# A hybrid decoder step on one core: norm statistics by token, another order of the first units, one more product pair, fewer passes for the sample tokens, and moved layer norm steps

## The chip, the core and the metric

The kernel runs on one core of one Trainium2 chip. The metric is the device time of one execution, in microseconds (us). In what follows PE is TensorE, DVE is VectorE, ACT is ScalarE, POOL is GpSimd and SP is SyncE, which here only issues loads and stores.

## What is computed

One layer of a decoder with four parallel branches, in fp32, over 1024 prompt tokens and 8 x 4 sample tokens (T = 1056 tokens, width 1024):

```python
h = rmsnorm(x, norm_g)
p = h @ w_in                                   # 1024 -> 16*512 + 8 + 4*1024 columns
# A: short gated convolution   B: retention, 4 heads, rotary q and k, head norm
# C: GLU, causal depthwise convolution of 31 taps, layer norm, swish
# D: mLSTM, 4 heads, exponential input gate, running-max stabiliser, head norm
y = x + (sum_n sigmoid(g_n(h)) * (o_n @ w_br[n])) @ w_out
out = rmsnorm(y, final_g)                      # and the new states of all branches
```

The samples carry their own states in, the prompt starts from zero, and all new states are outputs.

## The kernel before

**Numbers as two halves.** Every matmul operand is split into a high part (a copy rounded to fp32r, on ACT, line 1409 for weights) and a low part (the rest, by subtraction, on POOL, line 1739). A product is then three passes: high x high, high x low, low x high. The matrix of normalised tokens is `h_hi` and `h_lo`, 8 slices of channels by 1056 tokens.

**Start.** `x` comes in transposed, `xt`, in three blocks of 352 tokens. ACT squares it (line 1416), DVE (block 0, lines 1899 to 1903) or POOL (blocks 1 and 2, lines 1754 to 1758) adds up the 8 slices of channels, PE sums over partitions (`square_sums`, line 1045), ACT takes the root, DVE the reciprocal, and PE spreads that over all partitions (`spread_row`, line 1055). DVE multiplies (line 1911), ACT makes the high part (line 1427), DVE the low part (line 1884). `keep_busy` issues matmuls on constants between these steps.

**Units.** The input projection is done in units of 128 output channels. A unit is three blocks of 352 tokens, a block two halves of 12 matmuls (lines 1112 to 1114); the unit of the input and forget gates (`if`) has 16 small ones per block. A planner, `make_plan`, writes the order of everything: it counts half blocks, and a task stands at a number of half blocks within its phase. All engines walk the same list (`walk`), each in order and each doing only its own part, so that a task can make its engine wait while later work is queued behind it. The phases are: the gate unit and head 0 of the mLSTM (6 units, with the gate steps `m1` to `m7`, then the mask steps `mw` and `mws`), three more mLSTM heads, four retention heads, and a last one with the first GLU unit, a z unit and 4 plain gate units. During each phase the attention of the head before runs (`a`, `b`, `bs1`, `bs2`, `pn`, `pr`, `pt`): `a` transposes a chunk and makes scores, DVE masks them (line 2359), `b` (line 1282) multiplies them by the values, `pn` and `pr` normalise (line 2442), `pt` (line 1322) transposes back. `m1` is 9 transposes by matmul (line 1191), `m2` takes a logarithm on ACT, `m6` (lines 1218 to 1222) and a store and a broadcast load make the mask's row maxima, `mw` (line 2321) and `mws` (line 2329) the masks on DVE. The first `a` waits for all of them.

**Pairs.** The other input channels are done as 27 pairs of units: 7 products of half size (Winograd's form of Strassen's scheme) in place of 8, each in two parts, so 14 slots of 12 matmuls of 264 tokens (lines 1161 to 1163). Their sums are made on DVE, their sigmoids on ACT, and the weight sums on POOL. The operand sums of h (`comb`, `comb4`, lines 2161 to 2181) are made during the retention phases. Pair kinds are `cvcg` (GLU), `acau` and `abaz` (branch A), `cz` (branch C) and `g` (gates). In free slots DVE does the 120 steps of the 31-tap convolution (`tap`, line 2466), and from slot 263 of 378 on the layer norm (`ln0` to `ln3`, lines 2498 to 2534).

**End.** 32 branch units of 4 slices (`pblk`), summed into `acc`, then the final product by tiles of 128 tokens (lines 1367 to 1369): 8 prompt tiles and a ninth that covers the last 128 rows, of which only the 32 sample rows are stored. Each tile is added to x, normalised and stored.

Of the kernel before, what the change touches and what calls it, by code (L numbers as in the profile page):

```python
# [56 lines left out]
CK = BLK // 4  # L57
IFC, IFW = 8, 40
ORDER = (1, 3, 0, 2)
PLAIN_GATES = 4  # L60
# [12 lines left out]
def make_plan():  # L73
# [3 lines left out]
    def phase(group, tasks):  # L77
# [4 lines left out]
        if not first:  # L82

            blocks[:6] = [(u, b) for b in range(3) for u in range(2)]
# [66 lines left out]
    for x, step in zip((0, 1, 2, 4, 5, 6, 8, 9, 11, 13, 15, 17, 18, 20, 21), attention(7)):  # L151
# [5 lines left out]
    for k in range(4):  # L157
        tasks.setdefault(24 + 3 * k, []).append(("comb4", k))
# [30 lines left out]
    for what in (glu(1), None, conv_a(0), None, out_a(0), None, glu(2), None, conv_a(1), None, glu(3), None, out_a(1),  # L189
# [35 lines left out]
    for b in range(3):  # L225
        for late_by, step in ((0, "ln0"), (5, "lnm"), (6, "ln1"), (9, "ln1b"), (12, "lnv"), (13, "lns"), (15, "ln2")):
            tasks_at(at + 16 * b + late_by, (step, b))
    for g in range(4):
        tasks_at(at + 48 + 4 * g, ("ln3a", g))
        tasks_at(at + 50 + 4 * g, ("ln3", g))  # L230
    assert at + 50 + 12 <= 14 * 23 + 8, at
# [38 lines left out]
    emit_split(("plain", 1))  # L270
    emit_split(("plain", 0))
    start_steps = plan_out
    plan_out = []
    for s in first:
# [4 lines left out]
        if u + RING < n1:  # L279
            emit_split(("plain", u + RING))  # L280
        if u == n1 - 3:
            emit_split(("win", 0, 0))
        if u == n1 - 2:
            emit_split(("win", 0, 1))
            emit_split(("win", 0, 2))
        if u == n1 - 1:
            for i in range(3, 6):
# [4 lines left out]
    cycle = [4, 2 * r0, 2 * r0 + 1, 2 * r1, 2 * r1 + 1, 5]  # L292
# [92 lines left out]
def place(u, b):  # L385

    return 2 * b + u if u < 2 else 3 * u + b
# [151 lines left out]
def hybrid_step(nc, xT, xtok, ngain, wa, wg, wi, wb, wo, vec, fg, gbias, c1, c2, decay, rot, ah, chist, m0, st,  # L539
                y, sa_p, sa_s, sc_p, sc_s, o_p, o_s, om_p, om_s):  # L540
    ctx = ExitStack()
    with ctx:
# [51 lines left out]
        sq = [at(f"sq{i}", [P, KD, BLK], F32, acc_at + 4 * KD * BLK * i) for i in range(2)]  # L594
        rcol = at("rcol", [CK, 12], F32, acc_at + 8 * KD * BLK)
# [5 lines left out]
        buf_at = [x_at, x_at + 12 * T]  # L601
        zs_at = spot[0]
# [87 lines left out]
        lnsq = at("lnsq", [P, 4, BLK], F32, set_at)  # L690
# [29 lines left out]
        ident = cst[:, C_ID:C_ID + P]  # L720
        g_rows = nc.dram_tensor("g_rows", [4 * KD, P, T], F32, kind="Internal").ap()
# [3 lines left out]

        xt_in = [sem(f"xt_in{i}") for i in range(6)]
# [30 lines left out]
        ss_done = sem("ss_done")  # L757
        sqrt_done = sem("sqrt_done")
        pool_step = sem("pool_step")
        total = sem("total")  # L760
# [114 lines left out]

        def dst_of(item):
# [3 lines left out]
            if item[0] == "plain":  # L880
                return w_hi[item[1] % RING][:, :], w_lo[item[1] % RING][:, :]
# [68 lines left out]
        def _(sp):  # L950
# [8 lines left out]
            for i in range(6):  # L959
                b, k0 = i // 2, 4 * (i % 2)  # L960
                sp.dma_start(xt[:, b, k0:k0 + 4, :], xT[b, :, k0:k0 + 4, :]).then_inc(xt_in[i], 16)
                if i == 1:
                    sp.dma_start(ng[:, :], ngain).then_inc(ng_in, 16)
                    sp.dma_start(cst[:, :], c1).then_inc(ident_in, 16)
                    load(0, None)
                    load(1, None)
# [3 lines left out]
            load(2, 1)  # L970

            sp.wait_ge(row_ready, 3)
            sp.dma_start(cst2[:, :], c2).then_inc(late_in, 16)
            load(3, 0)
# [51 lines left out]
            for i in range(9):  # L1026
                r0 = i * P if i < 8 else T - P
# [1657 lines left out]
```

## Time and profile before

| | us |
|---|---|
| Median of 3 runs | 1505.76 (1505.31 to 1506.43) |
| The profiled execution | 1505.34, of which 1503.5 are the span of the profile |
| PE, DVE, ACT, POOL busy | 1475.7, 887.4, 498.6, 672.9 |

The share of the clock that PE was granted is 1 at 2.4 GHz and 0.5 at 1.2 GHz. A group of instructions has its own idle time and what ended it; the view of waits sums this by releaser. The chain of work is followed back from the last instruction to what released it at each step.

### The profile page before, as it was taken

To read this page: it belongs to the slowest core of one execution; us is meant where nothing else is said; L and a number is where in the kernel's file an instruction comes from. 1 tells how busy PE (TensorE), PEld (TensorE's weight loads), DVE (VectorE), ACT (ScalarE), POOL (GpSimd) and SP (SyncE) were. 2 spreads that over 40 slices of the span, in tenths; PEclk is the share of its full clock that TensorE was granted. 3 is DMA by queue.
4 is the path that set the end of the run, shared out by engine and by line. 5 is a ranking of instruction groups with operands and counts; after the bars stand their busy time and mean duration, and the time that the engine had idled before them with its cause. 6 is when DMAs were issued, how large, how long until landed. Compare 5 with 4: busy or idle time off the path is not lost.

```text
span 1503.5 us, 26633 instructions
## 1 busy us (share of the span) xinstructions
PE 1475.7 (98%) x10322; PEld 1436.6 (96%) x10322; DVE 887.4 (59%) x1770; ACT 498.6 (33%) x1010; POOL 672.9 (45%) x495
## 2 busy tenths in 40 slices
PE   7999999999999999999999999999999999999998
PEld 7999999999999999999999999999899999999786
DVE  5453342546766655448777877877666324785432
ACT  4432332323333334233333333333544422220321
POOL 5121212212131332387777776776667844662100
PEclk8999999999999999999999999999999999999999
DMA  4120212222121221322222221232222476755221
GB/s 163 61 99 29 87 35 81 75 70 67 52 89 45 72 77 50 114 65 90 72 102 89 89 89 68 62 99 86 87 87 100 144 235 202 232 159 158 100 86 72
DMA packets 64132, 144.41 MB, mean 96 GB/s; under 512 B 7800, under 2 KB 36488, under 8 KB 63880
## 3 DMA queue, kind: packets, MB, share of 16 engines
q1 hardware_dynamic: 56616, 116.12, 24.0%
q0 software_dynamic: 6192, 22.27, 4.1%
q10 hardware_dynamic: 1200, 4.33, 0.7%
q8 instruction: 82, 1.34, 0.4%
q14 instruction: 42, 0.34, 0.1%
HBM read 107.06 MB, written 35.64 MB: 95 GB/s over the span
## 4 chain that ended last, share of the span: by engine, by line
PE 92%; DVE 4%; POOL 1%; ACT 1%; issue 1%; DMA 0%; DVEq 0%; SPq 0%; ACTq 0%; POOLq 0%
PE bank L1161 11%; PE bank L1163 11%; PE bank L1162 11%; PE bank L1112 11%; PE bank L1114 10%; PE bank L1113 10%; PE bank L1179 4%; PE bank L1180 4%; PE bank L1181 4%; PE bank L1367 2%; PE bank L1368 2%; PE bank L1369 2%; PE sums_ps L1300 1%; PE sums_ps L1267 1%; PE sums_ps L1282 1%; PE sums_ps L1286 1%
## 5 line engine op out<-in xcount | busy, mean ns | idle before, releaser
L1112 PE MATMUL bank<-h_hi,w_hi 128*128 128x352 f32 x1008 | 335.2, 333 | 0.0
L1114 PE MATMUL bank<-h_hi,w_lo 128*128 128x352 f32 x1008 | 325.0, 322 | 0.0
L1113 PE MATMUL bank<-h_lo,w_hi 128*128 128x352 f32 x1008 | 324.4, 322 | 0.0
L1739 POOL TENSOR_TENSOR w_lo<-stage,w_hi 128x1024 fp32r<-128x1024 f32 x44 | 105.9, 2406 | 371.3 <-ACT w_hi L1409 371.2
L1739 POOL TENSOR_TENSOR t_lo<-stage,t_hi 128x512 fp32r<-128x512 f32 x140 | 185.9, 1332 | 135.5 <-ACT t_hi L1409 135.4
L1161 PE MATMUL bank<-h_hi,t_hi 128*128 128x264 f32 x864 | 246.4, 285 | 0.0
L1162 PE MATMUL bank<-h_lo,t_hi 128*128 128x264 f32 x864 | 245.5, 284 | 0.0
L1163 PE MATMUL bank<-h_hi,t_lo 128*128 128x264 f32 x864 | 245.0, 284 | 0.0
L1112 PEld LDWEIGHTS bank<-h_hi,w_hi 128*128 128x128 f32 x1008 | 190.1, 189 | 1.0
L1113 PEld LDWEIGHTS bank<-h_lo,w_hi 128*128 128x128 f32 x1008 | 190.6, 189 | 0.0
L1161 PE MATMUL bank<-c_hi,t_hi 128*128 128x264 f32 x648 | 185.7, 287 | 4.8 <-DVEq L2153 3.1
L1114 PEld LDWEIGHTS bank<-h_hi,w_lo 128*128 128x128 f32 x1008 | 189.9, 188 | 0.0
L1163 PE MATMUL bank<-c_hi,t_lo 128*128 128x264 f32 x648 | 184.7, 285 | 0.0
L1162 PE MATMUL bank<-c_lo,t_hi 128*128 128x264 f32 x648 | 184.0, 284 | 0.0
L2466 DVE SCALAR_TENSOR_TENSOR sums_ps<-ext,vc,sums_ps 128x1024 f32<-128x1024 f32 x116 | 149.0, 1284 | 44.5 <-ACT sums_ps L1654 40.9
L1409 ACT ACTIVATE t_hi<-stage 128x512 fp32r<-128x512 f32 x140 | 87.8, 630 | 226.3 <-PE bank L1181 100.2
L1162 PEld LDWEIGHTS bank<-h_lo,t_hi 128*128 128x128 f32 x864 | 162.5, 188 | 0.3
L1161 PEld LDWEIGHTS bank<-h_hi,t_hi 128*128 128x128 f32 x864 | 162.4, 188 | 0.3
L1163 PEld LDWEIGHTS bank<-h_hi,t_lo 128*128 128x128 f32 x864 | 162.4, 188 | 0.0
L1739 POOL TENSOR_TENSOR t_lo<-wsum,t_hi 128x512 fp32r<-128x512 f32 x81 | 109.2, 1350 | 83.1 <-ACT t_hi L1409 83.0
L1161 PEld LDWEIGHTS bank<-c_hi,t_hi 128*128 128x128 f32 x648 | 122.3, 189 | 6.1 <-DVEq L2153 3.4
L1179 PE MATMUL bank<-o_hi,t_hi 128*128 128x352 f32 x384 | 124.1, 323 | 0.0
(360 smaller groups left out, 2853.1 us busy)
## 6 DMA issues: line engine op xcount, KB each, us to landing
stage<-in_wa SPq DMA_DIRECT2D x64, 512.0 KB, 3.3
piece<-g_rows SPq DMA_DIRECT2D x96, 176.0 KB, 2.9
stage<-in_wg SPq DMA_DIRECT2D x32, 512.0 KB, 3.8
g_rows<-sgt SPq DMA_DIRECT2D x112, 132.0 KB, 1.8
o_raw<-o_rows SPq DMA_DIRECT2D x16, 528.0 KB, 6.5
stage<-in_wb SPq DMA_DIRECT2D x32, 256.0 KB, 2.8
xr<-in_xtok SPq DMA_DIRECT2D x9, 512.0 KB, 3.5
xt<-in_xT SPq DMA_DIRECT2D x6, 704.0 KB, 6.7
```

The source lines that it names most:

```text
L1112: pe.matmul(out, hi, h_hi[:, k, tok(b)], start=(k == 0), stop=False)
L1113: pe.matmul(out, hi, h_lo[:, k, tok(b)], start=False, stop=False)
L1114: mm = pe.matmul(out, lo, h_hi[:, k, tok(b)], start=False, stop=(k == KD - 1))
L1161: pe.matmul(out, hi, a_hi(k), start=(first and k == 0), stop=False, skip_group_check=True)
L1162: pe.matmul(out, hi, a_lo(k), start=False, stop=False, skip_group_check=True)
L1163: mm = pe.matmul(out, lo, a_hi(k), start=False, stop=(k == 3), skip_group_check=True)
L1179: pe.matmul(out, hi, o_hi[n][:, k, tok(b)], start=(k == 0), stop=False)
L1180: pe.matmul(out, hi, o_lo[n][:, k, tok(b)], start=False, stop=False)
L1181: mm = pe.matmul(out, lo, o_hi[n][:, k, tok(b)], start=False, stop=(k == 3))
L1409: act.activation(dst_of(item)[0], split_src(item), ACT.Copy).then_inc(hi_done, 1)
L1739: pool.tensor_tensor(lo, split_src(item), hi.bitcast(F32), ALU.subtract).then_inc(lo_done, 1)
L2466: own(dve.scalar_tensor_tensor(cc[g][:, 0:TP] if k == CW - 1 else conv_ps, ext[g % 2][:, k:k + TP], vc[:, g, V_CW + k:V_CW + k + 1], conv_ ...
```

## The change

- **Norm of x.** x is loaded a second time, by token (`xk`, chunks of 128, 128 and 96 tokens), ahead of `xt`. ACT squares and sums each chunk in one instruction; the sums on DVE and POOL and `square_sums` are gone. `spread_row` has 3 pieces instead of 4, for block 1 after the first `if` block and for block 2 after block 0 of unit 2.
- **First units.** Units 0, 1 and 2 are interleaved by block (before: 0 and 1); unit 2 gets a third weight buffer, in the still empty `qkv`.
- **Gate steps.** `m1`'s transposes are split into three of 3 chunks. The steps stand at half blocks 14 to 29 (before 10 to 24), the masks at 32 to 35 (before 28 to 32). The attention of head 0 starts at half block 2 with a stride of 1.5 (before 1 and 1.55).
- **Moved sums.** `comb` in the retention phases at half blocks 16 to 21 (before 3 to 19). In the last phase head 7's last steps, and `comb4`, come sooner.
- **Gates.** 2 plain gate units instead of 4; the other two are one more pair, the first of now 28.
- **Layer norm.** It starts at slot 252 of 392, with 20 slots per block of tokens (before 16), and one square buffer is split in two places. The convolution's steps are spread over the slots again.
- **Normalisation of heads.** Line 2442 becomes a `scalar_tensor_tensor` with a broadcast column.
- **Final product.** The sample tile is third, its high and low parts stand side by side as 64 columns of weights, and it has two passes instead of three.

```diff
-PLAIN_GATES = 4
+PLAIN_GATES = 2
-            blocks[:6] = [(u, b) for b in range(3) for u in range(2)]
+            blocks[:9] = [(u, b) for b in range(3) for u in range(3)]
-    gates = {10: [("m1",)], 11: [("m2",)], 14: [("m3",)], 15: [("m4",)], 19: [("m5",)], 22: [("m6",)], 24: [("m7",)]}
+    gates = {14: [("m0", 0)], 15: [("m0", 3)], 16: [("m0", 6), ("m1",)], 17: [("m2",)], 19: [("m3",)], 20: [("m4",)], 24: [("m5",)],
+             27: [("m6",)], 29: [("m7",)]}
     for c in range(0, CH, 2):
-        gates[28 + c // 2] = [("mw", c), ("mw", c + 1)]
-    gates[32] = [("mws",)]
+        gates[32 + c // 2] = [("mw", c), ("mw", c + 1)]
+    gates[35].append(("mws",))
...
-            phase(mlstm(1), spread(attention(0), 1, 1.55))
+            phase(mlstm(1), spread(attention(0), 2, 1.5))
...
-            for i, x in enumerate((3, 7, 11, 13, 16, 19)):
+            for i, x in enumerate((16, 18, 19, 20, 20, 21)):
                 tasks.setdefault(x, []).append(("comb", h - 1, i))
             for c in range(3):
-                tasks.setdefault((20, 22, 23)[c], []).append(("comb_split", h - 1, c))
+                tasks.setdefault((22, 23, 23)[c], []).append(("comb_split", h - 1, c))
...
-    for x, step in zip((0, 1, 2, 4, 5, 6, 8, 9, 11, 13, 15, 17, 18, 20, 21), attention(7)):
+    for x, step in zip((0, 1, 2, 4, 5, 6, 8, 9, 11, 13, 15, 16, 17, 18, 19), attention(7)):
...
-        tasks.setdefault(24 + 3 * k, []).append(("comb4", k))
+        tasks.setdefault((20, 22, 24, 26)[k], []).append(("comb4", k))
...
-    for what in (glu(1), None, conv_a(0), None, out_a(0), None, glu(2), None, conv_a(1), None, glu(3), None, out_a(1),
+    for what in (None, glu(1), None, conv_a(0), None, out_a(0), None, glu(2), None, conv_a(1), None, glu(3), None, out_a(1),
...
-        for late_by, step in ((0, "ln0"), (5, "lnm"), (6, "ln1"), (9, "ln1b"), (12, "lnv"), (13, "lns"), (15, "ln2")):
-            tasks_at(at + 16 * b + late_by, (step, b))
+        for late_by, step in ((0, "ln0"), (6, "lnm"), (7, "ln1"), (10, "ln1b"), (14, "lnv"), (15, "lns"), (17, "ln2")):
+            tasks_at(at + 20 * b + late_by, (step, b))
...
+            by_token(0)
+            by_channel(0)
+            sp.dma_start(cst[:, :], c1).then_inc(ident_in, 16)
+            sp.dma_start(ng[:, :], ngain).then_inc(ng_in, 16)
+            load(0, None)
+            by_channel(1)
+            load(1, None)
+            by_token(1)
+            by_channel(2)
+            load(2, 0)
+            by_channel(3)
+            by_token(2)
...
             pe.wait_ge(ones_set, 1)
-            keep_busy(20)
-            square_sums(0)
-            keep_busy(3)
+            keep_busy(24)
             spread_row(0)
-            keep_busy(14)
-            square_sums(1)
+            keep_busy(22)
...
+            def square(b, j):
+                act.wait_ge(xk_in[3 * b + j], 16)
+                n, c = XCH[j], 3 * b + j
+                act.activation(xk[b % 2][0:n, j, :], xk[b % 2][0:n, j, :], ACT.Square,
+                               accum_out=rcol[0:n, c:c + 1]).then_inc(sq_done, 1)
...
-                    own(dve.tensor_scalar(rt[0:r, c, 0:P], rt[0:r, c, 0:P], mv[0:r, c, 0:1], rstd[0:r, c:c + 1],
-                                          ALU.subtract, ALU.mult))
+                    own(dve.scalar_tensor_tensor(rt[0:r, c, 0:P], rt[0:r, c, 0:P], mv[0:r, c, 0:1],
+                                                 rstd[0:r, c:c + 1].to_broadcast([r, P]), ALU.subtract, ALU.mult))
...
+        by_turn = (0, 1, CH) + tuple(range(2, CH))
...
+                        if by_turn[i] == CH:
+                            pe.matmul(out[0:2 * NS, :], f_two[:, k, :], hi, start=(k == 0), stop=False)
+                            mm = pe.matmul(out[0:2 * NS, :], f_two[:, k, :], lo, start=False, stop=(k == KD - 1))
+                            continue
```

## Rows read from the trace of the kernel before

**Rows 1.** The page, part 1: busy time, share of the span, instructions.

```profile
PE 1475.7 (98%) x10322; PEld 1436.6 (96%) x10322; DVE 887.4 (59%) x1770; ACT 498.6 (33%) x1010; POOL 672.9 (45%) x495
```

**Rows 2.** Waits of PE: line, releaser, us in total, times, longest.

```profile
PE sums_ps L1045 <- DVE sq L1903: 4.3, 1, 4.3
PE sums_ps L1045 <- POOL sq L1758: 3.6, 1, 3.6
PE bank L1161 <- DVEq L2153: 3.1, 1, 3.1
PE sums_ps L1282 <- DVE sw L2359: 3.1, 4, 1.0
PE sums_ps L1322 <- DVEq L2445: 1.9, 1, 1.9
PE bank L1161 <- DVE part L2026: 1.7, 2, 1.1
```

**Rows 3.** Stretches: length, busy time (instructions) by engine, granted clock, DMA share, GB/s.

```profile
25.00:30.00 5.00, 5.00 (x28) 4.03 (x27) 1.45 (x4) 1.52 (x2) 4.84 (x4) 0.66 0.30 105
50.00:55.00 5.00, 5.00 (x23) 5.00 (x23) 0.20 (x1) 2.67 (x3) 1.21 (x1) 0.68 0.33 107
1060.00:1070.00 10.00, 6.86 (x43) 6.31 (x42) 8.67 (x16) 2.11 (x5) 3.87 (x4) 0.85 0.35 107
```

**Rows 4.** Stretches of one plain unit, one pair, one final tile, columns as above.

```profile
625.70:637.10 11.40, 11.40 (x73) 11.40 (x73) 0.00 (x0) 2.86 (x5) 5.87 (x4) 1.00 0.42 141
955.60:976.00 20.40, 20.40 (x171) 20.40 (x170) 16.44 (x27) 6.67 (x14) 14.61 (x12) 1.00 0.23 66
1452.60:1463.80 11.20, 11.20 (x50) 9.05 (x49) 3.97 (x5) 2.51 (x4) 0.00 (x0) 1.00 0.27 94
```

**Rows 5.** The chain at the start: start us, us, what.

```profile
1.20 5.30 DMA xt<-in_xT
...
8.93 0.53 DVE sq L1901
9.49 2.56 DVE sq L1903
...
25.26 0.20 PE bank L1098
```

**Rows 6.** Instructions at the start in order of time: start us, us, instruction.

```profile
4.77 1.38 ACT L1416 ACTIVATE sq<-xt 128x1408 f32<-128x1408 f32 x1 [2.34 <-DMA xt<-in_xT]
...
9.32 2.34 POOL L1739 TENSOR_TENSOR w_lo<-stage,w_hi 128x1024 fp32r<-128x1024 f32 x1 [7.12 <-ACT w_hi L1409]
...
16.48 4.02 DVE L1911 SCALAR_TENSOR_TENSOR xt<-xt,ng,sums_ps 128x352 f32<-128x352 f32 x8 [2.60 <-PE sums_ps L1055]
```

**Rows 7.** Instructions of the gate and mask steps, in order of time.

```profile
46.98 2.10 PE L1191 MATMUL sums_ps<-sel,gif 40*128 40x8 f32 x18
...
53.73 1.28 ACT L1502 ACT_TABLE_LOAD   x1
...
75.82 1.03 PE L1222 MATMUL sums_ps<-dms,cst 4*128 4x8 f32 x8
...
88.77 2.43 DVE L2321 SCALAR_TENSOR_TENSOR wt<-wt,aa,cst 128x128 f32<-128x128 f32 x8
...
102.00 0.71 DVE L2329 SCALAR_TENSOR_TENSOR wts<-sums_ps,aa,cst 32x32 f32<-32x32 f32 x4 [0.51 <-DVE wt L2321]
...
106.50 0.27 PE L1263 MATMUL sums_ps<-cst,qkv 128*128 128x128 f32 x1
```

**Rows 8.** The chain in a retention phase.

```profile
402.81 0.71 DVE c_raw L2161
```

**Rows 9.** The chain in the abaz pair.

```profile
1059.95 2.38 DVE sums_ps L2522
```

**Rows 10.** Stores of y, two stretches: KB each, median us from issue to landing.

```profile
out_y<-yo ACTq DMA_DIRECT2D x1, 512.0 KB, 2.6
...
out_y<-yo ACTq DMA_DIRECT2D x1, 128.0 KB, 1.9
```

More of the change, by code:

```diff
@@ L269, in make_plan @@
     push_loads()
-    emit_split(("plain", 1))
-    emit_split(("plain", 0))
+    for n in range(3):
+        emit_split(("plain", n))
     start_steps = plan_out
@@ L385, in place @@
 def place(u, b):
[L387 removed]
+    return 3 * b + u if u < 3 else 3 * u + b
 def done_counts():
@@ L723, in hybrid_step @@
         nm_row = nc.dram_tensor("nm_row", [CH * HEADS, P], F32, kind="Internal").ap()
+        xk_in = [sem(f"xk_in{i}") for i in range(9)]
         xt_in = [sem(f"xt_in{i}") for i in range(6)]
@@ L1039, in keep_busy @@
                     pe.matmul(bank[4][:, 0:P], ones[:, :], ones[:, :], start=True, stop=True)
-            def square_sums(b):
-                pe.wait_ge(total, b + 1)
-                for j in range(4):
-                    mm = pe.matmul(tb[0:CK, 4 * b + j:4 * b + j + 1], sq[b % 2][:, 0, CK * j:CK * j + CK], ones[:, 0:1],
-                                   start=True, stop=True)
-                mm.then_inc(ss_done, 1)
             def spread_row(b):
@@ L1053, in spread_row @@
                 pe.wait_ge(recip_done, b + 1)
-                for j in range(4):
-                    mm = pe.matmul(rows[b][:, CK * j:CK * j + CK], rcol[:, 4 * b + j:4 * b + j + 1].to_broadcast([CK, P]),
-                                   ident[0:CK, 0:CK], start=True, stop=True)
+                for j in range(3):
+                    n = XCH[j]
+                    mm = pe.matmul(rows[b][:, P * j:P * j + n], rcol[0:n, 3 * b + j:3 * b + j + 1].to_broadcast([n, P]),
+                                   ident[0:n, 0:n], start=True, stop=True)
                 mm.then_inc(row_ready, 1)
             pe.wait_ge(ones_set, 1)
-            keep_busy(20)
-            square_sums(0)
-            keep_busy(3)
+            keep_busy(24)
             spread_row(0)
-            keep_busy(14)
-            square_sums(1)
+            keep_busy(22)
             last = {}
@@ L1427, in upper @@
                 act.activation(h_hi[:, ks, tok(b)], xt[:, b, ks, :], ACT.Copy).then_inc(hh_done, 1)
-            act.wait_ge(ones_set, 4)
+            act.wait_ge(ones_set, 5)
             own(act.activation(ss[:, 0, 1:2], eps[:, :], ACT.Sqrt))
-            square(0)
-            square(1)
+            for j in range(3):
+                square(0, j)
+            root(0)
             split(0)
-            root(0)
-            square(2)
-            square(3)
+            upper(0, 0)
             split(1)
-            upper(0, 0)
             upper(0, 1)
+            square(1, 0)
             upper(0, 2)
-            square(4)
+            square(1, 1)
+            square(1, 2)
             root(1)
-            square(5)
+            split(2)
+            square(2, 0)
             upper(1, 0)
+            square(2, 1)
             upper(1, 1)
+            square(2, 2)
+            upper(1, 2)
             root(2)
-            upper(1, 2)
             for i in range(3):
@@ L1914, in _ @@
                         mul.then_inc(hn_dve, 1)
-                lower(b, 0)
-                lower(b, 1)
-                if b == 1:
-                    reciprocal(2)
-                lower(b, 2)
-                if b == 0:
-                    reciprocal(1)
+                for i in range(3):
+                    lower(b, i)
+                if b < 2:
+                    reciprocal(b + 1)
             dve.wait_ge(const_in, 48)
```

198 lines of the change are left out of this document (96 added, 102 removed).

## The prediction

> **What bounds the kernel now.** Read part 1 of the page first: TensorE is busy for 1475.7 of 1503.5 us, and no other engine for more than 59% of it [rows 1]. So time is won in two ways only: fewer TensorE columns, or shorter TensorE waits. The waits by releaser come next: two waits on the norm at the start of 4.3 and 3.6 us, 3.1 on VectorE's scores in four places, 3.1 in one piece and 1.7 in two (the longer 1.1) at products of pairs, and 1.9 at an attention head's transpose [rows 2]. The third view is the stretches with the granted clock: at 25 to 30 us, 50 to 55 us and 1060 to 1070 us it is 0.66, 0.68 and 0.85, that is 2.4 GHz falls to 1.2 GHz for part of them [rows 3]. Each follows idleness or tiny matmuls: the first the wait for the norm of block 1, the second the 18 matmuls of 8 columns of the gate step [rows 7], the third the 3.1 us wait. The loss is (1 - clock) x length: 1.7, 1.6 and 1.5 us. Last, what a unit costs: a plain unit takes 11.4 us, a pair 20.4 us, a tile of the final product 11.2 us, all at full clock [rows 4].
>
> **1. Start: 12.5 us less.** Before, the first product starts at 25.26 us [rows 5]. After, the order of loads decides. Two loads of 704 KB land 1.74 us apart, with the first there at 4.77 and the second at 6.50 [rows 5, 6], so the flow begins near 3.0 and takes 2.5 us per 1000 KB. Token chunks of 512, 512 and 384 KB land at 4.3, 5.6, 6.5; x by channel at 8.2 and 10.2; the first ring weight at 11.5; block 1 by token at 12.8 to 15.0, by channel at 16.7 and 19.7. A square of 1408 columns takes 1.38 us [rows 6], one of 1024 by its length 1.0, with its sum about 1.1, so the third ends at 7.8, the root at 8.0. The 48 warm-up matmuls end near 8.7, the row is spread by 9.5. VectorE's eight multiplies take 4.02 us [rows 6]: 13.5. ScalarE splits unit 1's weight at 12.2 to 13.2, and GpSimd's half of it runs 13.3 to 15.7. Here I chose. VectorE's first lower half wants to start at 13.5, while GpSimd is subtracting. In the trace such an add of 352 columns took 2.56 us from 9.49 on, beside a GpSimd subtraction of 9.32 to 11.66, where the one before it took 0.53 [rows 5, 6]. I take the blocked value: the lower half ends at 16.6, the first product starts at 16.7, 8.6 us sooner; free, 14.7. The Trainium skill (SBUF — State Buffer, Who interferes with whom) says that a VectorE instruction with two SBUF inputs and a GpSimd one that reads SBUF exclude each other, the first to issue going first; the 2.56 us agrees. By that rule the 0.2 us between 13.3 and 13.5 decides 2 us.
> Nothing after it should stop TensorE: with three units per block there are 2.6 + 3.9 + 3.9 us of products to hide the 8 us of the next block's norm, and blocks 1 and 2 come at 28.6 and 38.9, h_lo ready at 27.7 and 36.0. So the clock loss of 1.7 us at 25 to 30 goes. The gate transposes in three parts of 6 tiny matmuls (2.1 us in all, as before) between full products: the 1.6 us at 50 to 55 go as well. The matmuls for square sums go, and the spread has 9 pieces for 12: 0.6 us. Together 8.6 + 1.7 + 1.6 + 0.6 = 12.5. Bounds 9 (the wait of 14.3 to 16.7 halves the clock, and a late load) to 14.5.
>
> **2. The gate steps come closer together: 2.8 us more.** A half block is 1.93 us. Between the second and third gate step there were three halves, now two; ScalarE there does a split and two table loads of 1.28 us [rows 7], about 4.5 us in all against 3.9: 0.7 us of waiting, and 0.3 at the next, where VectorE now has the sigmoid of the z unit ahead of it. Then the mask: the sixth step's matmuls end at 76.85, the broadcast of the row maxima is in for VectorE at 88.77, the sample mask is done at 102.7, and the first attention tile starts at 106.50 [rows 7]. That is 25.9 us of chain in 29.7 us of products: 3.8 spare. After, the sixth step moves from half 22 to 27 and the tile from 37 to 38: 11 halves instead of 15, about 22.2 us. The chain loses a copy (0.65) and perhaps the blocked instruction in it (about 1.9): 23.4 to 25.3. TensorE waits 1.2 to 3.1 us there; I take 1.8, since GpSimd's next subtraction starts only near the chain's end. Behind this wait stand all of TensorE's units, so it is paid in full. Sum 0.7 + 0.3 + 1.8 = 2.8; bounds 1 to 6 (with a clock fall). Start and gates: 9.7 us won.
>
> **3. Sums of h moved in the retention phases: 2.1 us.** In three phases VectorE does a sum of 0.71 us [rows 8] between rotation and the scores for which TensorE waits [rows 2]. At halves 16 to 21 it lies in VectorE's idle time before the transposes. 3 x 0.71 = 2.1; bounds 1 to 2.2, since the rotation's own blocked add stays.
>
> **4. Last attention head: 2.0 us.** The transpose waited 1.9 us for VectorE's normalisation [rows 2], which had begun late because ScalarE did a split and a table load ahead of its root, and whose first instruction GpSimd blocked. Now the root is at half 16, ahead of the split, one half sooner; the transpose comes two halves sooner. From 1.9 us of wait about zero stays: ready at 601, wanted at 601.3. Bounds 0 to 2.2. The other form of that instruction (scalar_tensor_tensor) I count as nothing: 9 per head behind other work.
>
> **5. Two gate units become a pair: 2.5 us.** 2 x 11.4 - 20.4 = 2.4 to 2.5 [rows 4]. Its sums and sigmoids lie beside other work: VectorE was busy 16.44 of 20.4 us in a full pair [rows 4].
>
> **6. Layer norm: 6.0 us.** At 1059.95 VectorE's reciprocal of 2.38 us [rows 9] and four multiplies sit in the abaz pair before the parts that free TensorE's banks: 3.1 us waited [rows 2] and 1.5 us of clock [rows 3], about 5.0 with the restart of the queue. Later the mean of the third block costs 0.6, since VectorE's sum for it stands right behind a reciprocal, and in the cz pair the last step of the layer norm stands ahead of a product's sum, 1.1 waited [rows 2] and 0.3 of restart. Together about 7. After, by the slots, block 0 lies in the acau and the gate pair, block 1's reciprocal at slot 9 of abaz, three slots sooner. Adding up VectorE's queue there (4.2 us of reciprocal and multiplies, 0.43 each for some ten operations, 1.6 for the next sum) the last bank is freed 26.0 us after the pair's start, and wanted at 25.7: 0.3 us. In the gate pair VectorE has 20.5 us of work in 20.4: another 0.3 to 0.8. I leave 1.0 of 7.0. Bounds 2 (b below) to 7.
>
> **7. Final product: 3.0 us.** The sample tile has 32 matmuls instead of 48; a matmul takes 11.2 / 48 = 0.233 us [rows 4]: 3.7 us. It also goes third, so the last store is 512 KB and not 128: 2.6 against 1.9 us to landing [rows 10], 0.7 back. VectorE's four more instructions (0.7 each) hide under 7.4 us of products.
>
> **Sum:** 9.7 + 2.1 + 2.0 + 2.5 + 6.0 + 3.0 = 25.3 us. The profiled execution took 1505.34 us (1503.5 span and 1.8 around it), so 1480.0 by it; the median shown is 0.4 above: 1480.4.
>
> **Rivals.**
> (a) The attention tile's wait decides. The chain of step 2 is blocked (25.3 us), the idleness of 3 us brings the clock down as the 3.1 us wait did [rows 2, 3], and the wait at 14.3 us does so too: 1.3 + 1.6 + 1.7 more, and about 1485. Against it: the 1.9 us wait at the last head left the clock alone.
> (b) VectorE is still too full around abaz: the layer norm moves its wait from one pair to the next and keeps 4 to 5 of the 7 us, 1484. For it: 79 to 80% busy in full pairs before a layer norm step is added.
> (c) VectorE goes first in the collision at 13.5 and the mask chain is not blocked: 2 + 1 less, 1477.
> (d) On the other side: VectorE becomes the bound of the pairs. From 20.4 us of its work per pair each further us is paid once in each of 28 pairs; the fullest had 16.44 [rows 4]. Taps now sit closer from the first pair on and keep a pair from recovering; 21.4 us in every pair would cost 28 us and give about 1508. The same taps in more slots speak against it.
> (e) The norm by token brings nothing: x is read twice, and if the 1408 KB ahead of x by channel cost what the squares' sums did, the first product stays at 25: about 1489. Against it: before, two thirds of the 25 us went to squares' sums on three engines, after both first loads were in at 6.5 [rows 5].
>
> **Chances.** Forecast (1478 to 1482.5) 0.45; (a) 0.17; (b) 0.14; (c) 0.13; (e) 0.06; (d) 0.02; several small ones at once, 1486 to 1492, 0.03. The range 1475.5 to 1487.5 takes in all but some 0.12 of it. Faster by over 0.2% (what a measurement of this kernel can tell from none, 3 us) 0.97, within 0.01, slower 0.02.
>
> **What would show it.** First product near 16.7 us and no clock below 1 before 60 us. A wait at the first attention tile, with VectorE's sample mask as releaser. No wait of scores over 0.6 us in the three phases; none at the last head's transpose. In the abaz pair under 1 us. 28 pairs of 20.4 us and 41 units ahead of them. The last store issued 2.6 us before the end. Wrong would be the whole if VectorE or a split became a releaser of many small TensorE waits in the pairs.

## The result and the profile after

The changed kernel takes 1498.43 us (median of 4 runs, 1498.03 to 1499.24), the kernel before 1506.1 beside it (median of 4): a ratio of 0.9949, interval 0.9936 to 0.9961. It is faster by 7.7 us, where 25.3 were forecast. The profiled execution took 1499.24 us with a span of 1497.5, 6.0 less than the profiled one before; the table below takes these 6.0 us apart.

Where the 25.3 us went is read from the starts of TensorE's stages in the two traces. A minus sign means that the stretch became longer.

| stretch | forecast, us won | measured |
|---|---|---|
| start and gate steps (to the tenth plain unit, 164.4 before, 158.7 after) | 9.7 | 5.7 |
| retention phases (the next units to 599.4 before, 592.2 after) | 2.1 | 1.5 |
| last attention head (to the end of the unit after z, 614.2 and 611.4) | 2.0 | -4.4 |
| two gate units as a pair (22.9 us against 20.4) | 2.5 | 2.5 |
| pairs beyond 20.4 us each (27 pairs before, 28 after) | 6.0 | -2.1 |
| final product | 3.0 | 2.8 |

Three of the six lines came out within 0.6 us, the first fell 4.0 short, and the last head and the pairs ended on the other side of zero. The pairs' line is the time from the first product of pairs to the last (562.4 and 584.9 us) less 20.4 for each pair. The page, part 1, of after, which answers to [rows 1]:

```profile
PE 1468.2 (98%) x10318; PEld 1427.2 (95%) x10318; DVE 901.7 (60%) x1779; ACT 504.3 (34%) x1031; POOL 669.9 (45%) x495
```

TensorE has 7.5 us less of busy time, and is still busy for 98% of the span. Its waits by releaser (line, releaser, us in total, times, longest), which answer to [rows 2]:

```profile
PE bank L1182 <- DVEq L2160: 5.1, 1, 5.1
PE sums_ps L1345 <- DVEq L2452: 4.6, 2, 3.7
PE bank L1119 <- DVE h_lo L1902: 2.5, 1, 2.5
PE sums_ps L1079 <- DVE rcol L1907: 2.4, 1, 2.4
PE bank L1182 <- DVE part L2033: 1.3, 2, 0.7
PE sums_ps L1305 <- DVE sw L2366: 1.2, 4, 0.3
PE sums_ps L1305 <- ACTq L1576: 1.2, 1, 1.2
...
PE sums_ps L1220 <- DVEq L2234: 0.8, 1, 0.8
```

The wait at the abaz pair, 3.1 us before, is 5.1 (first line), and the one at the last head's transpose, 1.9 before, is 3.7 in one piece (second line; the other 1.0 of it is the first head's). The scores' waits fell from 3.1 to 1.2, as forecast. The granted clock (columns as in [rows 3]) is whole in the two stretches at the start where it fell before the change, and falls behind the two long waits:

```profile
10.00:30.00 20.00, 16.70 (x119) 15.35 (x118) 15.71 (x22) 13.72 (x22) 5.72 (x4) 1.00 1.02 375
50.00:60.00 10.00, 9.66 (x61) 9.01 (x60) 0.91 (x4) 5.41 (x7) 4.76 (x2) 1.00 0.17 55
...
595.00:605.00 10.00, 7.05 (x29) 6.60 (x30) 5.12 (x10) 1.52 (x3) 6.08 (x5) 0.66 0.30 105
...
1060.00:1072.00 12.00, 6.86 (x33) 6.14 (x32) 8.47 (x15) 0.97 (x3) 7.63 (x8) 0.72 0.44 136
```

That is 3.4 us lost to 1.2 GHz at either place. Two stretches of after in order of time show what VectorE did there. c_lo is the lower half of a sum of h, w_lo that of a unit's weight, t_lo that of a pair's. The last head:

```profile
591.60 6.24 DVE L2449 SCALAR_TENSOR_TENSOR rt<-rt,mv,rstd 128x128 f32<-128x128 f32 x9
592.12 0.54 POOL L1789 DMA_DIRECT2D out_o_p<-cn  x1
592.68 1.35 POOL L1809 TENSOR_TENSOR c_lo<-c_raw,c_hi 128x528 fp32r<-128x528 f32 x1
...
593.98 2.40 POOL L1770 TENSOR_TENSOR w_lo<-stage,w_hi 128x1024 fp32r<-128x1024 f32 x1
...
597.95 1.97 PE L1345 MATMUL sums_ps<-cst,rt 128*128 128x128 f32 x8 [3.66 <-DVEq L2452]
```

The nine normalising instructions take 6.24 us; in the first seven heads the same nine take 2.44. One by one they are 0.35, 0.35, 2.06, 2.43, and five of 0.34. Two are stretched: the third ends 0.16 us after c_lo, the fourth 0.16 us after w_lo. By the profile the third begins at 592.13, 0.55 us ahead of c_lo; starts on GpSimd are rough, so that c_lo is what held it is inferred from where it ends. The abaz pair:

```profile
1055.30 0.42 DVE L2052 TENSOR_TENSOR ta<-bank,ta 128x264 f32<-128x264 f32 x1
1055.64 1.17 DVE L2054 TENSOR_TENSOR ta<-part,ta 128x264 f32<-128x264 f32 x1
...
1058.68 1.52 DVE L2505 TENSOR_TENSOR lnsq<-cc,cc 128x352 f32<-128x352 f32 x1
1060.12 1.58 DVE L2506 TENSOR_TENSOR lnsq<-cc,cc 128x352 f32<-128x352 f32 x1
1061.74 1.47 DVE L2508 TENSOR_TENSOR lnsq<-lnsq 128x352 f32<-128x352 f32 x1
```

```profile
1055.04 1.48 POOL L1770 TENSOR_TENSOR t_lo<-stage,t_hi 128x512 fp32r<-128x512 f32 x1
1058.52 2.80 POOL L1770 TENSOR_TENSOR t_lo<-stage,t_hi 128x512 fp32r<-128x512 f32 x2 [2.00 <-ACT t_hi L1436]
1061.29 1.54 POOL L1770 TENSOR_TENSOR t_lo<-wsum,t_hi 128x512 fp32r<-128x512 f32 x1
```

The three adds of the layer norm's block 2 take 1.5 us each; the adds of blocks 0 and 1 take 0.52. Beside them GpSimd makes three lower halves. In the first two rows a multiply with one operand in PSUM (bank) runs its 0.42 us in the middle of a lower half, and the next, of the same size with both in SBUF, takes 1.17.

The whole trace of after says the same. Of VectorE's tensor_tensor instructions with both operands in SBUF, 93 ran beside an elementwise instruction of GpSimd and 65 of these were stretched by over 0.15 us; of 134 that ran clear of it, none was. With an operand in PSUM 364 ran beside it, and none was stretched by more than 0.02 us (counted over instructions that occur at least three times, against their usual time).

### The profile page after: what moved, and what is told of

It is laid out like the page before. It is cut to its first block, busy times and chain, and to the rows that moved or that the text cites. A ratio compares the mean times of both kernels' runs of the same rounds, so it can differ in the third digit from the quotient of the medians.

```text
span 1497.5 us, 26690 instructions
## 1 busy us (share of the span) xinstructions
PE 1468.2 (98%) x10318; PEld 1427.2 (95%) x10318; DVE 901.7 (60%) x1779; ACT 504.3 (34%) x1031; POOL 669.9 (45%) x495
## 4 chain that ended last, share of the span: by engine, by line
PE 88%; DVE 6%; DMA 2%; ACT 2%; issue 1%; POOL 1%; SPq 0%; DVEq 0%; ACTq 0%; POOLq 0%
PE bank L1182 12%; PE bank L1184 11%; PE bank L1183 11%; PE bank L1133 10%; PE bank L1135 9%; PE bank L1134 9%; PE bank L1200 4%; PE bank L1201 4%; PE bank L1202 4%; PE bank L1394 1%; PE bank L1396 1%; PE bank L1395 1%; PE sums_ps L1290 1%; PE sums_ps L1305 1%; PE sums_ps L1309 1%
## 5 line engine op out<-in xcount | busy, mean ns | idle before, releaser
L1133 PE MATMUL bank<-h_hi,w_hi 128*128 128x352 f32 x960 | 320.1, 333 | 0.0
L1135 PE MATMUL bank<-h_hi,w_lo 128*128 128x352 f32 x960 | 309.8, 323 | 0.0
L1134 PE MATMUL bank<-h_lo,w_hi 128*128 128x352 f32 x960 | 309.1, 322 | 0.0
L1182 PE MATMUL bank<-h_hi,t_hi 128*128 128x264 f32 x896 | 255.5, 285 | 0.0
L1183 PE MATMUL bank<-h_lo,t_hi 128*128 128x264 f32 x896 | 254.6, 284 | 0.0
L1184 PE MATMUL bank<-h_hi,t_lo 128*128 128x264 f32 x896 | 254.1, 284 | 0.0
L1133 PEld LDWEIGHTS bank<-h_hi,w_hi 128*128 128x128 f32 x960 | 181.1, 189 | 1.1
L1134 PEld LDWEIGHTS bank<-h_lo,w_hi 128*128 128x128 f32 x960 | 181.6, 189 | 0.0
L1135 PEld LDWEIGHTS bank<-h_hi,w_lo 128*128 128x128 f32 x960 | 180.9, 188 | 0.0
L1183 PEld LDWEIGHTS bank<-c_lo,t_hi 128*128 128x128 f32 x672 | 127.3, 189 | 0.5 <-issue 0.2
```

The lines of the kernel that those rows point to most:

```text
L1133: pe.matmul(out, hi, h_hi[:, k, tok(b)], start=(k == 0), stop=False)
L1134: pe.matmul(out, hi, h_lo[:, k, tok(b)], start=False, stop=False)
L1135: mm = pe.matmul(out, lo, h_hi[:, k, tok(b)], start=False, stop=(k == KD - 1))
L1182: pe.matmul(out, hi, a_hi(k), start=(first and k == 0), stop=False, skip_group_check=True)
L1183: pe.matmul(out, hi, a_lo(k), start=False, stop=False, skip_group_check=True)
L1184: mm = pe.matmul(out, lo, a_hi(k), start=False, stop=(k == 3), skip_group_check=True)
```

## The experiments

The theory after the result: GpSimd's subtractions hold VectorE's instructions that have both operands in SBUF, and the changed kernel puts two groups of them at places where GpSimd works and TensorE waits. All edits are to the changed kernel. Gains are counted from its median of 1498.43 us unless another is named; times of the executions of one kernel spread by 1 to 5 us. Readings of single rows are from the profiled execution of each run.

**e1: the last head's transposes later.**

```
-    ... 13, 15, 16, 17, 18, 19), attention(7)):
+    ... 13, 15, 16, 17, 20, 21), attention(7)):
-    tasks.setdefault((20, 22, 24, 26)[k], []).append(("comb4", k))
+    tasks.setdefault((22, 23, 25, 27)[k], []).append(("comb4", k))
```

> The changed kernel with one edit: the two transpose steps of the last attention head lie at half blocks 20 and 21 of their phase, as before, instead of 18 and 19 (the sums of its four tiles follow at 22, 23, 25, 27, since their buffers overlap). Its normalisation stays at half 16. Theory (the steps came sooner than VectorE can normalise there, since GpSimd's c_lo and w_lo hold it): TensorE arrives at 597.8, VectorE is done at 597.84, so the wait of 3.7 us falls under 0.3 and the 6.8 us at 1.2 GHz behind it go too (3.0 us): 1498.4 - 6.5 = 1491.9. Rival 1 (the clock fall does not come from this wait): 3.7 less, 1494.7. Rival 2 (the later sums of tiles hold the first pair): the same gain less 1 to 3 us of a new wait at 622, 1493 to 1495.

Measured: 1493.93 us (1493.22 to 1497.77), 4.5 less where the theory said 6.5; this is in the range of rival 2. In the trace the nine instructions still took 6.30 us, nobody waited for them, and the pairs begin at 616.9 instead of 622.9: 6.0 us, wait and clock fall. Behind that rival 2 came too, but smaller than its 1 to 3 us: the first pair's wait for L2033 grew from 0.6 to 1.3 us. That the median gained less than the trace may come from executions of the changed kernel in which the clock did not fall there (e9); it is not shown.

**e2: the form of the instruction.**

```
-    own(dve.scalar_tensor_tensor(rt..., rt..., mv[0:r, c, 0:1], rstd[0:r, c:c + 1].to_broadcast([r, P]), ...))
+    own(dve.tensor_scalar(rt..., rt..., mv[0:r, c, 0:1], rstd[0:r, c:c + 1], ALU.subtract, ALU.mult))
```

> The changed kernel with one edit: the nine normalising instructions per head in their form of before (tensor_scalar with two scalars per partition, instead of scalar_tensor_tensor with a broadcast SBUF operand). Theory (the place beside GpSimd's c_lo and w_lo decides, not the form; in the kernel before one tensor_scalar of this group took 2.07 us there): nine pieces of the last head still take 4 to 6.3 us, wait 3.7 and clock fall stay, 1498.4 within 1 us. Rival (the second SBUF operand is what gets blocked): the nine take 2.4 to 3 us, end at 594.5, wait about 0.5, no clock fall: 1498.4 - 6.2 = 1492.

Measured: 1497.74 us. The row of the nine in its trace:

```profile
591.43 6.10 DVE L2449 TENSOR_SCALAR rt<-rt,mv,rstd 128x128 f32<-128x128 f32 x9
```

6.10 against 6.24, two of them 2.01 and 2.38, where 2.06 and 2.43 stood. The form of the instruction makes no difference here, as the prediction had counted it.

**e3: the layer norm off the abaz pair.**

```
+    late_by += (0, 5 if step == "ln2" else 0, 3)[b]
```

and the closing steps three slots later.

> The changed kernel with the layer norm moved off the abaz pair: the last step of block 1 (reciprocal and four products) five slots later, in the gate pair behind, and all steps of block 2 and the closing steps three slots later. Theory (VectorE's work of the layer norm in the abaz pair makes the wait of 5.1 us at 1060 and the 6.8 us at 1.2 GHz): both go, 8.5 us, and up to 1 us comes back in the gate pair: 1490 to 1491. Rival (VectorE is too full in any pair there): a wait of 2 to 4 us stands in the gate pair instead, with its clock fall: 1494 to 1497.

Measured: 1497.22 us, 0.2 above the rival's range, and by its mechanism: the wait for the abaz pair's bank (L2160) is gone, and 4.1 us are waited for a product's sum in the gate pair behind, with a clock fall. The reciprocal and the adds of block 2 now stand next to each other there, and the adds again run beside GpSimd (columns: start, us, instruction):

```profile
1063.19 1.10 DVE L2506 TENSOR_TENSOR lnsq<-cc,cc 128x352 f32<-128x352 f32 x1
1064.04 1.37 POOL L1758 TENSOR_TENSOR wsum<-wsum,stage 128x512 f32<-128x512 f32 x1
1064.22 1.58 DVE L2507 TENSOR_TENSOR lnsq<-cc,cc 128x352 f32<-128x352 f32 x1
...
1065.83 1.47 DVE L2509 TENSOR_TENSOR lnsq<-lnsq 128x352 f32<-128x352 f32 x1
```

So it was not the abaz pair as such. The first of the three (1.10 for 0.52) ran beside GpSimd's instruction of 1062.38 to 1063.90, which is an add of two half weights, so not only subtractions hold VectorE.

**e4: the three adds alone.**

```
+    late_by += 3 if (step, b) == ("ln0", 2) else 0
```

> The changed kernel with a single step moved: the channel sums of block 2 (three VectorE adds) three slots later, out of the abaz pair; the reciprocal and the products of block 1 stay at its slot 9. Theory (the collision decides: three adds of 1.5 us beside GpSimd's lower halves, 0.52 elsewhere): the queue is 4.6 us shorter, the wait of 5.1 falls to 0.5 to 1.0, no clock fall, 1490.5 to 1491.5, and the three adds take 0.52 each or are blocked where nobody waits. Rival (the reciprocal and products of 4.2 us fill the queue and the adds count only with their own 1.6): a wait of about 3.5 us and the clock fall stay, 1496.8.

Measured: 1493.78 us (1492.93 to 1496.6), 4.6 less where 7 to 8 were forecast; in the trace the 28 pairs take 5.7 us less, with the clock whole. At their new place the adds ran 0.55, 0.51 and 0.52 us, and the reciprocal with its products, unmoved, leaves a wait of 0.4. The matmul that needs the adds now waits 1.3 us, which accounts for the gap between the trace and the forecast, not for that between the median and the trace.

**e13: GpSimd's work cut, nothing moved.**

```
+    n = 16 if item in (("plain", NU - 1), ("win", 21, 4), ("win", 21, 5), ("win", 21, 6)) else hi.shape[-1]
-    pool.tensor_tensor(lo, split_src(item), hi.bitcast(F32), ALU.subtract)
+    pool.tensor_tensor(lo[..., 0:n], split_src(item)[..., 0:n], hi[..., 0:n].bitcast(F32), ALU.subtract)
```

> The changed kernel with four of GpSimd's subtractions cut to 16 columns: w_lo of the last plain unit (2.40 us, 593.98 in the trace of after) and the three t_lo of 1058.5 to 1062.8 (1.3 to 1.5 us each). Nothing of VectorE's or TensorE's work and no place of a step is changed; the lower halves of those weights are left out but for 16 columns. c_lo (1.35 us, ahead of w_lo) stays. Theory (GpSimd's subtractions hold VectorE's instructions): at the last head the third of the nine pieces is still held by c_lo (2.0 us), the fourth falls from 2.43 to 0.35, the wait from 3.7 to 1.8 us; the three adds of block 2 fall from 1.5 to 0.52 each, the wait from 5.1 to about 2.2; with the clock falls of 6.8 us gone or halved 1498.5 - 4.9 - 3 to 6 = 1488 to 1491. Rival (VectorE is slow there for itself, or beside ScalarE): pieces and adds keep their length, 1498.5.

Measured: 1490.46 us (the kernel before 1505.82 beside it), 8 less. The rows:

```profile
592.16 4.17 DVE L2450 SCALAR_TENSOR_TENSOR rt<-rt,mv,rstd 128x128 f32<-128x128 f32 x9
...
593.24 1.36 POOL L1810 TENSOR_TENSOR c_lo<-c_raw,c_hi 128x528 fp32r<-128x528 f32 x1
594.54 0.29 POOL L1771 TENSOR_TENSOR w_lo<-stage,w_hi 128x16 fp32r<-128x16 f32 x1
```

```profile
1054.62 0.53 DVE L2506 TENSOR_TENSOR lnsq<-cc,cc 128x352 f32<-128x352 f32 x1
1055.06 0.54 DVE L2507 TENSOR_TENSOR lnsq<-cc,cc 128x352 f32<-128x352 f32 x1
1055.64 0.53 DVE L2509 TENSOR_TENSOR lnsq<-lnsq 128x352 f32<-128x352 f32 x1
```

One of the nine is still held (2.07), beside the c_lo that was left; the one held by w_lo is free (0.34). The adds are 0.53. The waits are 1.6 and 2.2 us where 1.8 and 2.2 were expected; behind the second the clock still fell, and 1.7 us were lost. This shows the cause: the same VectorE work stood in the same places, and only GpSimd's was taken away. It agrees with the Trainium skill (SBUF — State Buffer, Who interferes with whom), by which a VectorE instruction with two SBUF inputs contends with a GpSimd one that reads SBUF, and the one that issues second is fully blocked; the page names tensor_scalar among those that can contend, and in e2 it was held.

**e7: the layer norm's spacing undone.** Stride 16 for 20, offsets (0, 5, 6, 9, 12, 13, 15).

> The changed kernel with the layer norm spaced as before (16 steps from block to block, offsets 0, 5, 6, 9, 12, 13, 15), in the new order of pairs. The reciprocal of block 1 then lies at slot 3 and the adds of block 2 at slot 4 of the abaz pair. What the prediction said (the wider spacing brings 6 us): 1504. Theory (what counts is whether a step lies ahead of a bank's release beside GpSimd's subtractions, not the spacing): waits of 2 to 4 us in that pair instead of 5.1 and less of a clock fall, 1495 to 1499.

Measured: 1501.85 us (11 executions, 1499.72 to 1504.89; the profiled one took 1503.2), between the two expectations and above the theory's. There are two waits in gate pairs, both with a clock fall: 3.5 us at a product (1022), behind a reciprocal and adds held for 1.12, 1.59 and 1.47 us, and 3.1 at a matmul of the variance (1065), whose sums VectorE brings late; no run takes the second apart further. So the new spacing did win 3.4 us in the new order of pairs, and the order itself had lost more: beyond 20.4 us each, the pairs take 11.6 us before, 17.5 with the old spacing in the new order, 13.7 in the changed kernel.

**e11: the place of the added pair.**

```
-    for what in (None, glu(1), None, ... out_a(3), None, None, None, out_c(0), ...
+    for what in (glu(1), None, ... out_a(3), None, None, None, None, out_c(0), ...
```

> The changed kernel with a single edit: the added pair of gate units stands before the two cz pairs, not at the head of the pairs. Taps and layer norm then fall on the pairs as before the change: of the layer norm the abaz pair holds the mean, squares and variance of block 0, and both the reciprocal and the adds of the next block come in the gate pair behind it. Theory (where the steps meet the abaz pair's releases decides; the place of the added pair put them there): 28 pairs take 571.2 plus 5 to 9 us instead of plus 13.7: 1490 to 1494. Rival (in any pair the reciprocal with the adds behind it makes a wait of 3 to 5 us and a clock fall): 1497 to 1500.

Measured: 1494.87 us, 3.6 less and 0.9 above the theory's range. The 28 pairs take 571.2 plus 10.0 us: 3.7 less than in the changed kernel, by one line in a list, but 1 us more than expected. A wait of 2.6 us stays in the gate pair behind the abaz pair.

**e12 and e14: what that wait is.** e12 is e11 with the three edits of e5, e6 and e1 (sums of tiles at 22, 23, 24, 26); e14 is e12 with the adds of blocks 1 and 2 two slots later.

> The first three edits of the combination (start, gates, last head) with the added pair before the cz pairs in place of the layer norm's moved steps. Theory: 1498.4 - 11.2 and the gain of the pair's place as the run with that edit alone shows it, 4 to 8 us: 1479 to 1483. Rival (the collision comes back in the gate pair): 1486.

> The combination with the added pair ahead of the cz pairs, and the channel sums of the layer norm's blocks 1 and 2 two slots later. In the combination without it the three adds of block 1 take 1.4 to 1.6 us each behind the reciprocal, beside GpSimd, and make a wait of 2.9 us at 1031 with 3.4 us at 1.2 GHz behind it. Theory: two slots later the adds stand behind the products' sums, so the wait falls under 0.5 and the clock stays: 1484.2 - 4.3 = 1479.9. Rival (GpSimd works there as well, and the adds are held two slots later at the next bank): 1483 to 1484.

Measured: 1484.17 and 1480.34 us. e12 lies 1.2 us above the theory's range: the place of the pair brought 3.7 us and not 4 to 8, since the wait of 2.6 us and its clock fall stay. There the adds stand ahead of the sum that TensorE waits for:

```profile
1028.92 1.41 DVE L2508 TENSOR_TENSOR lnsq<-cc,cc 128x352 f32<-128x352 f32 x1
...
1030.26 1.60 DVE L2509 TENSOR_TENSOR lnsq<-cc,cc 128x352 f32<-128x352 f32 x1
...
1031.89 1.47 DVE L2511 TENSOR_TENSOR lnsq<-lnsq 128x352 f32<-128x352 f32 x1
...
1033.62 0.43 DVE L2036 TENSOR_TENSOR part<-bank,part 128x264 f32<-128x264 f32 x1 [0.25 <-DVE lnsq L2511]
```

In e14 both sums of that step are done at 1031.1, the adds behind them are still held (1.06, 1.61 and 1.50 us), and there is no wait: a held instruction costs only what stands behind it.

**e5: the norm of block 2 later.** `spread_row(2)` after (0, 1) for (2, 0); ScalarE's `upper(1, i)` ahead of `square(2, i)`.

> The changed kernel with two edits in the start: TensorE spreads the norm of block 2 after the gate unit's product of block 1 instead of before it, and ScalarE copies the three parts of block 1's h ahead of the squares of block 2 instead of between them. Theory (the wait of 2.7 us at 28.9 is the norm of block 2, asked for 2.6 us before it can be there, since its token rows land at 24.6 to 28 us): the wait goes, at most 0.3 us stands at the new place: 1498.4 - 2.4 = 1496.0. Rival (the loads of x, now taken twice, bound the start: the products of block 2 find their h_lo late instead): the wait reappears there, 1498 to 1498.4.

Measured: 1498.5 us, by the time alone no gain, and the number is the rival's. By the trace the theory holds: the wait is gone and none stands in its place, every later stage begins 2.4 us sooner (the pairs at 620.5 for 622.9), and the profiled span is 1495.1 for 1497.5. Two things in e9 can hide this in the median, and no run separates them: the clock at the last head, and that the wait itself is 0.9 us and not 2.4 in some executions.

**e9: the changed kernel again.**

> The changed kernel unedited, as a base on the same chip for the three runs beside it: 1498.4 within 1.5 us, with the waits of 2.7 us at 28.9, 4.0 at 594 and 5.4 at 1060 in their places.

Measured: 1499.09 us, but 1495.85 to 1499.82. The 1495.85 is the profiled run, and in it the wait at the last head is there (3.6 us) without the fall of the clock. The wait for the norm of block 2 is 0.9 us there and not the 2.7 that was expected: behind the wait of 2.5 us for the first product, which both traces have, the clock fell in this one, which lost 1.7 us, and TensorE came to the norm that much later (columns as in [rows 3]):

```profile
18.00:24.00 6.00, 6.00 (x31) 4.63 (x30) 2.88 (x6) 2.51 (x4) 1.72 (x1) 0.72 1.04 403
```

The tenth plain unit begins at 158.6 us in it and at 158.7 in after, so this fall cost nothing as long as the norm was late anyway. The stretch 590 to 605 us in after, in e6 and in e9:

```profile
590.00:605.00 15.00, 11.34 (x56) 10.61 (x55) 9.86 (x18) 5.58 (x10) 9.51 (x8) 0.77 0.30 110
```

```profile
590.00:605.00 15.00, 11.06 (x63) 10.51 (x62) 8.62 (x14) 2.75 (x6) 9.64 (x8) 0.89 0.32 124
```

```profile
590.00:605.00 15.00, 11.36 (x72) 10.82 (x72) 9.79 (x18) 5.46 (x9) 9.61 (x8) 1.00 0.29 111
```

Clock 0.77, 0.89 and 1.00 of full behind waits of 3.7, 3.9 and 3.6 us: 3.4, 1.7 or 0 us lost. A single edit of 2 us can be lost in that unless the trace is read.

**e6: gate steps.** m3, m4 at 20, 21 for 19, 20; the first head's steps at 2, 4, 5, 7, ... for 2, 3, 5, 6, ..., its transposes at 22 and 23.

> The changed kernel with the third and fourth gate step one half block later (20, 21), the scores' step of the first attention tile one half later behind its first step (4 for 3), and the transposes of that head one half later (22 for 21, 23 stays). Theory (three small waits of the closer gate phase: 0.8 us at 59.3 for two activation tables in a row, 1.2 at 103.6 for ScalarE's table between the mask's exponential and the tile's sigmoid, 1.0 at 152.4 for the normalisation): all three go with their restarts, 1498.4 - 3.3 = 1495.1. Rival (the chain of the masks is the bound, and the later third step pushes it): 0.8 and 1.0 go, but 1 to 2 us appear at the first tile: 1497.

Measured: 1494.57 us, 3.9 less (3.3 were forecast). All three waits are gone and none came; the tenth plain unit begins 3.5 us sooner. The pairs begin 4.6 us sooner, in which the shorter clock fall of its profiled run has a part (1.7 us less, the rows under e9).

**e8: the sums of h at their old halves.**

> The changed kernel with the combinations of h in the three retention phases at their halves of before. Prediction's term and theory agree: a sum of 0.70 us lies between the rotation and the scores again, three times: +1.9 to 2.1, 1500.4, with the waits for scores at about 1.3 instead of 0.66 us. Rival (the moved sums were hidden anyway, and the shorter wait has another cause): 1498.4.

Measured: 1500.80 us. The scores' waits are 3.1 us again, three of them 0.96 for 0.34 us, and the pairs begin 2.0 us later: the term is right.

**e10: the four together.** e5, e6, e1's transposes (sums of tiles at 22, 23, 24, 26), the adds of block 2 three slots later and its other steps one.

> Four edits of the changed kernel together: the norm of block 2 spread one product later with ScalarE's copies ahead of its squares; gate steps 3 and 4, the first tile's scores and that head's transposes one half block later; the last head's transposes at 20 and 21 with its sums of tiles at 22, 23, 24, 26; the layer norm's channel sums of block 2 three slots later and its other steps one later. Theory (four separate waits, each by work of VectorE or ScalarE asked for too soon; the gains add): by the starts of the pairs 2.4 + 3.6 + 5.2, and 6.5 in the layer norm: 1498.4 - 17.7 = 1480.7, clock at 1.2 GHz nowhere between 20 us and the end. Rival (a gain in one place moves GpSimd's subtractions in the next into a new collision): one of the four comes back, 1484 to 1487.

Measured: 1481.24 us (1480.93 to 1481.77), ratio to the kernel before 0.9837, interval 0.9823 to 0.985. Its clock and busy time from 20 us to the end of the last product, and its waits:

```profile
20.00:1475.00 1455.00, 1447.08 (x10212) 1408.61 (x10210) 887.52 (x1756) 490.72 (x1010) 664.83 (x484) 1.00 0.30 97
```

```profile
PE bank L1123 <- DVE h_lo L1906: 2.5, 1, 2.5
PE bank L1186 <- DVE part L2037: 2.1, 2, 1.4
PE sums_ps L1309 <- DVE sw L2370: 1.2, 4, 0.3
...
PE bank L1186 <- DVEq L2164: 0.4, 1, 0.4
```

The clock is whole in this stretch but for its first 2 us, the end of a fall behind the first product's wait that the mean hides. The gains add as the traces had them: 17.9 us less than the changed kernel beside it, 17.7 expected, while the medians of e1, e4, e5 and e6 alone add up to 12.9. e14 is as fast or a little faster, 1480.34 us, 0.983 (0.9816 to 0.9843): a version 18 us below the changed kernel and 25.5 below the one before. That this is the 1480.4 that was forecast is chance: it took further edits that the prediction did not have.

## Why the prediction was wrong

1. **Start: mechanism right, about 4 us too much.** The clock falls at 25 and 50 us went, as forecast. The first product came at 17.9 us, not 16.7: the collision with w_lo came as priced (the first lower half took 3.24 us for 3.1), but the third chunk of rows had landed at 7.7 us for 6.5. The step that failed is "nothing after it should stop TensorE". The spread of block 2's norm stands behind the third unit's product of block 0, and TensorE reaches it at 29.2, while the prediction timed only the products' need of h_lo. The rows of after:

```profile
24.64 1.06 ACT L1442 ACTIVATE xk<-xk 128x1024 f32<-128x1024 f32 x1 [2.29 <-DMA xk<-in_xtok]
...
31.57 0.91 PE L1079 MATMUL sums_ps<-cst,rcol 128*128 128x128 f32 x6 [2.38 <-DVE rcol L1907]
```

The three chunks of block 2 land at 24.6, 26.3 and 28.1 us. The prediction's 2.5 us per 1000 KB from 3.0 us on would give 23.7 for the third (8260 KB with those ahead of it), so the rate was too fast as well: measured, it is 3.0. ScalarE's copies of block 1's h stand between the squares and add to it. e5 takes 2.4 us of it back. About 1 us of the 4 is not traced.
2. **Gate steps: size nearly right, places partly wrong.** 0.7, 0.3 and 1.8 us were forecast. The third step waited 0.8. At the first tile's first step nothing was waited, since ScalarE's last exponential of the mask was done as TensorE came (101.05, 101.32): the chain from the sixth step's matmuls to the sample mask took 21.4 us, and 23.4 to 25.3 had been forecast. The table load from exponential to sigmoid behind it made 1.2 us at the scores one step later; before the change that place had 0.8. The rival (a) with a clock fall did not come. Not on the list was a third, 1.0 us at that head's transposes, which had also come closer. That is 2.2 us more of waits for 2.8.
3. **Sums of h: right.** 1.5 to 2.0 us for 2.1.
4. **Last head: wrong in sign, 6.4 us.** The step "ready at 601, wanted at 601.3" took the blocked first instruction for a thing of the old place ("whose first instruction GpSimd blocked"), and moved the normalisation without asking what GpSimd does at the new one. There c_lo and w_lo run back to back for 3.7 us, two instructions are held instead of one, and the transposes were asked for two halves sooner on top: TensorE came at 594.3, and VectorE was done at 597.8. Wait 3.7 us and clock 3.4. e1 and e13 show it. That the form counts as nothing was right (e2).
5. **Two units as a pair: 2.5 right, its side effect missed.** The added pair stands at the head, and all taps and the layer norm move against the pairs. The prediction took the new slots for its sum, but never priced what that order would cost. What the pairs take beyond 20.4 us each:

| us | order as before | added pair at the head |
|---|---|---|
| old spacing of the layer norm | 11.6 (the kernel before, 27 pairs) | 17.5 (e7) |
| new spacing | 10.0 (e11) | 13.7 (the changed kernel) |

The order cost 3.7 us with the new spacing and 5.9 with the old.
6. **Layer norm: 6.0 us forecast, 1.6 to 3.8 won by the spacing (the table), and 2.1 lost with the order.** The step "0.43 each for some ten operations, 1.6 for the next sum" is the one that failed. It used the durations of unblocked rows in the fullest pair, and gave the sum for block 2 (three adds) 1.6 us; it took 4.6, and two more multiplies 1.57 and 1.17 for 0.42 each. That is 4.9 us in the queue, and the wait came out at 5.1 for 0.3. The same law stood in the prediction for the start and was not carried here, though the kernel before shows it in these adds too: block 2's took 1.11, 1.61 and 1.49 us there, block 1's 0.52 each. Rival (b), VectorE too full around abaz at 1484, was nearest, and too mild.
7. **Final product: right.** The sample tile took 7.4 us (1415.89 to 1423.29) for 11.2; the store cost about what was said.

The signs named under "What would show it" on the scores and the number of pairs held, the one on the clock at the start in the profile of after, but not in that of e9 (0.72 from 18 to 24 us). The first product came 1.2 us late and no wait stood at the first attention tile. The signs on the last head and the abaz pair failed, and that is where the time was.

## What to carry to other kernels

When a step is moved, look up what the neighbour engine does at the new place, and price each VectorE instruction with both operands in SBUF at up to its own length plus what is left of GpSimd's instruction there, not at its length in a quiet row (the fourth piece of the last head: 0.34 and 2.27 left of w_lo, and it took 2.43). Put such instructions behind what another engine waits for; then they may be held for free. An operand in PSUM takes an instruction out of it (none of 364 was held here). When several small schedules are moved at once, a gain of 20 us can shrink to 8 by two waits of 4 us, so look for the longest waits first and read each edit of 2 us from the trace, not from the time.

## What the runs showed of the hardware

- A held VectorE instruction gets in between two GpSimd instructions that stand back to back, and the next one is held anew: three adds of 0.52 us beside three lower halves took 1.52, 1.58 and 1.47, and the three GpSimd ones 1.29 to 1.55. Here each of the three paid anew.
- tensor_scalar with one tensor and two per-partition scalars was held as long (2.01 and 2.38 us) as scalar_tensor_tensor with a broadcast second operand (2.06 and 2.43); unheld both take 0.33 to 0.35. GpSimd issuing DMAs (0.54 to 0.60 us each) held none of the pieces beside it in the first head of after (0.35 each at 151.1 to 151.9).
- After a wait of 3.6 to 3.9 us at the last head the clock was down in some executions and not in others, and for different lengths: means of 0.77, 0.89 and 1.00 over the same 15 us. After the 2.5 us wait for the first product it was whole in after and fell in e9, the same kernel, where 1.7 us were lost. The wait of 5.1 us at 1060 had a fall behind it in every profile that had that wait, and so had the ones of 2.6 us in e11 and e12 and of 2.2 us in e13.
